# Gates of tokens 0 to 127 through a table in DRAM, written by accumulating scatter DMAs, in a kernel of two transformer blocks with PEER experts

## The chip, the cores and the metric

The kernel runs on one core of a Trainium2 chip. The time is the device time in microseconds (us), as a median of several runs; a profiled execution gives the trace. Engines are named as in the profile: PE (TensorE; PEld is its weight load), DVE (VectorE), ACT (ScalarE), POOL (GpSimd) and SP (SyncE, which here issues the loads of weights).

## The reference

256 tokens of width 1024 pass a first block (an attention and a gated linear recurrence, an FFN, a gate) and a second block: a mixer of two attentions, and then a PEER layer, which is the part that matters here.

```python
def peer_ffn(xn, w_peer_q, sub_keys, expert_u, expert_v):
    xt = xn.reshape(T, D)
    qh = (xt @ w_peer_q).reshape(T, PEER_HEADS, 2, PEER_HALF)      # 8 heads
    s = jnp.einsum('thpd,hpnd->thpn', qh, sub_keys)                # 128 keys a half
    sv, si = lax.top_k(s, PEER_TOPK)                               # 16
    cand = sv[:, :, 0, :, None] + sv[:, :, 1, None, :]
    cand_idx = si[:, :, 0, :, None] * PEER_NKEYS + si[:, :, 1, None, :]
    best, pick = lax.top_k(cand, PEER_TOPK)
    expert_idx = jnp.take_along_axis(cand_idx, pick, axis=-1)      # of 16384 experts
    gates = jax.nn.softmax(best, axis=-1)
    ...
    hval = jnp.einsum('cd,chkd->chk', xc, expert_u[ic])
    a = gc * jax.nn.gelu(hval, approximate=False)
    return jnp.einsum('chk,chkd->cd', a, expert_v[ic])
```

So each token has 8 x 16 = 128 pairs of an expert and a gate. Within a head a token's 16 experts differ; two heads may pick the same one, and their gates then add up.

## The kernel before

**Weights.** All weights come as units of 128 x 1024 float32 (0.5 MB), in one fixed order (plan, line 38). SP loads unit u into raw[u % 4] as soon as DVE is done with the unit four before it (weights, line 465). ACT rounds it to wh (high, line 1736), DVE makes the rest wl = raw - wh (low, line 655; the subtraction is line 665), and PE multiplies with both halves. ACT and DVE work some three units ahead of PE (LOOK = 3; in the expert_u phase DVE does low of two units ahead).

**The PEER layer, dense part.** Tokens 0 to 207 (TN = 208) are multiplied with all 16,384 experts: 128 blocks of expert_u, in the order ORDER, n = 0 to 127. The gelu of each product is multiplied by a gate that is zero where the token did not pick the expert, and the result goes through the 128 blocks of expert_v. The gates stand in one tile, gates[128, 128, 208]: the partition is the index j in a block, then comes the block i, then the token. The gelus of the first NP = 50 blocks are put in this tile while the gates don't exist yet (early, line 3121; gelu, line 2266).

**The gates.** DVE finds each token's picks beside the query weights and the first 50 blocks of expert_u: four sorts of the sub-keys for each half of the tokens (q = 0 and 1; line 1452), then for each q the pairs (pairs, ranks, at_rank: lines 1462 to 1518), which end in ij (i and j of each pick), and gain and gain_sum, which make the gates bst. ACT does the exp and copies keys for it at fixed blocks (at_keys, line 2299). Between them slot() (line 1442) does low of one weight unit. PE turns ij and bst over (line 3137), and from block 51 on a chunk of four tokens is built beside each block: DVE and ACT make one-hot tiles oj and oi (128 picks x 128, oi scaled by the gate), and PE multiplies them for each token, which gives all 16,384 gates of it in a bank (line 3155). DVE and ACT carry them from the bank into the tile gates, multiplied by the gelus that are there (lines 1636 and 2348). 208 tokens are NC = 52 chunks, at blocks 51 to 102. Blocks after 50 have their gelu multiplied by the part of the gates built so far (gated, line 1583; built, line 379).

**The few tokens.** Tokens 208 to 255 don't go through all experts. Their picks and gates are copied to DRAM and back (few_picks, pick), and POOL fetches rows of expert_u and expert_v with 2 x 48 indirect DMAs of 128 rows of 4 KB each (line 645). A row fetch j waits until fetch j - 3 was used, as there are three buffers. DVE uses them in slots (slot_taken, line 1596), a dot product or a multiply-add of 1024 elements. slots_taken (line 435) writes the places out:

```python
at = {GATED - 1 - 3 * k: SOON - 1 - k for k in range(SOON)}
for n in range(GATED, NE - 2, 2):
    at[n] = len(at)
```

That is slot 0 at block 57, then each third block to block 102, and each second from block 103; the rest in the expert_v phase. DVE works in the order in which these loops write it, so a slot whose row isn't there holds up all that stands behind it.

## Time and profile before

| | |
|---|---|
| median of 3 runs | 1323.21 us (1322.51 to 1324.47) |
| the profiled execution, its own time | 1321.23 us |
| its span in the trace | 1319.4 us |
| PE busy | 1298.7 us (98%) |
| DVE busy | 1069.2 us (81%) |
| ACT busy | 821.6 us (62%) |
| POOL busy | 226.9 us (17%), 151 instructions |
| DMA | 292.73 MB, mean 222 GB/s |

Times within the trace count from the start of its span. A matmul is pipelined, so the time of a stretch is read from the starts of the instructions in it and not from the sum of their durations. The span on POOL of a DMA that it issues is the time in which POOL builds it, not the transfer.

### The profile page before, as it was taken

Reading aid. Unit: us, or ns where it says so; the run is one execution under the profiler, and the core shown is the slowest. Engines: PE = TensorE matmul, PEld = TensorE weight load, DVE = VectorE, ACT = ScalarE, POOL = GpSimd, SP = SyncE. Lnnn points to the kernel's source line nnn. Section 1 sums busy time; section 2 is a strip of 40 time slices with the busy share of each in tenths; the row PEclk is TensorE's granted clock in tenths of the full one; section 3 lists DMA queues with packets and bytes.
Section 4 is the critical chain, followed back from the end, with each engine's and each line's share of the span. In section 5 each row is a group of like instructions: output and inputs, shape, how many; then the busy total and the mean of one; then the engine's idle time right before and its main releaser. Section 6 shows DMA issues by size and latency. Waiting matters only on the chain.

```text
span 1319.4 us, 21754 instructions
## 1 busy us (share of the span) xinstructions
PE 1298.7 (98%) x8061; PEld 1200.7 (91%) x8061; DVE 1069.2 (81%) x1974; ACT 821.6 (62%) x1601; POOL 226.9 (17%) x151
## 2 busy tenths in 40 slices
PE   8999999999999999999899999999999999999998
PEld 6998888888889888889899999999999999999995
DVE  6867776666677675778899889999999989988985
ACT  6886555555556555455466888888666555555553
POOL 3002030000000000000000021100334436545610
PEclk9999999999999999999899999999999999999999
DMA  6533365555535344654656655565788999999972
GB/s 228 182 120 136 113 223 192 186 187 189 183 136 176 128 144 166 232 190 155 183 202 220 208 211 208 200 210 200 271 304 325 366 344 361 369 364 342 349 281 91
DMA packets 82603, 292.73 MB, mean 222 GB/s; under 512 B 10217, under 2 KB 10873, under 8 KB 82242
## 3 DMA queue, kind: packets, MB, share of 16 engines
q1 hardware_dynamic: 68450, 240.70, 52.8%
q0 software_dynamic: 14048, 50.64, 10.4%
q8 instruction: 65, 1.06, 0.3%
q14 instruction: 40, 0.33, 0.1%
HBM read 288.95 MB, written 2.34 MB: 221 GB/s over the span
## 4 chain that ended last, share of the span: by engine, by line
PE 86%; DVE 7%; ACT 3%; DMA 3%; issue 2%; POOL 0%; SPq 0%; POOLq 0%; DVEq 0%; ACTq 0%
PE bank L2409 84%; DMA raw<-in_wts 3%; DVE wl L665 2%; PE bank L2507 1%; ACT wh L1748 1%; DVE rows L1604 1%; PE bank L2495 1%; DVE oi L1580 0%; DVE gates L1636 0%; DVE oj L1576 0%; DVE gates L1588 0%; ACT kdz L1754 0%; DVE St L855 0%; ACT oi L2329 0%; ACT oi L2333 0%
## 5 line engine op out<-in xcount | busy, mean ns | idle before, releaser
L2409 PE MATMUL bank<-hTb,wh 128*128 128x416 f32 (+3 forms) x2768 | 827.5, 363 | 3.4 <-DVE wl L665 3.2
L2409 PE MATMUL bank<-hTb,wl 128*128 128x208 f32 (+2 forms) x2584 | 652.7, 264 | 0.0
L665 DVE TENSOR_TENSOR wl<-raw,wh 128x1024 fp32r<-128x1024 f32 x429 | 523.9, 1228 | 133.8 <-ACT wh L1748 131.5
L1748 ACT ACTIVATE wh<-raw 128x1024 fp32r<-128x1024 f32 x429 | 449.8, 1057 | 205.5 <-PE bank L2409 118.3
L2409 PEld LDWEIGHTS bank<-hTb,wh 128*128 128x128 f32 (+1 forms) x2768 | 506.2, 189 | 26.0 <-issue 4.8
L2409 PEld LDWEIGHTS bank<-hTb,wl 128*128 128x128 f32 (+1 forms) x2584 | 492.7, 191 | 4.8
L2409 PE MATMUL bank<-wh,hTb 128*128 128x512 f32 (+2 forms) x552 | 175.0, 398 | 1.9 <-DVE hTb L699 1.9
L2409 PEld LDWEIGHTS bank<-wh,hTb 128*128 128x128 f32 (+1 forms) x552 | 102.2, 187 | 24.7 <-DVE wl L665 2.1
L645 POOL DMA_INDIRECT rows<-in_v_rows,pick x48 | 105.6, 2200 | 92.0 <-DVE acc L1615 76.8
L645 POOL DMA_INDIRECT rows<-in_u_rows,pick x48 | 74.3, 1548 | 229.5 <-DVE dots L1604 226.8
L2409 PE MATMUL bank<-wl,hTb 128*128 128x512 f32 (+2 forms) x276 | 100.3, 389 | 0.0
L563 POOL TENSOR_TENSOR st<-st,mhalf 128x1 f32<-128x1 f32 (+2 forms) x15 | 13.1, 877 | 501.5 <-DVE st L672 252.5
L1754 ACT ACTIVATE low_half<-bank 128x208 fp32r<-128x208 f32 x77 | 26.6, 345 | 62.5 <-PE bank L2409 62.1
L2409 PEld LDWEIGHTS bank<-wl,hTb 128*128 128x128 f32 (+1 forms) x276 | 51.6, 187 | 10.5
L1615 DVE SCALAR_TENSOR_TENSOR acc<-rows,factor,acc 128x1024 f32<-128x1024 f32 x46 | 58.9, 1280 | 0.0
L1604 DVE CUSTOM_DVE_ANT_0 rows<-rows,xr 128x1024 f32<-128x1024 f32 x48 | 58.6, 1222 | 0.0
L2409 PE MATMUL bank<-oi,oj 128*128 128x128 f32 x416 | 55.2, 276 | 0.0
L2409 PEld LDWEIGHTS bank<-oi,oj 128*128 128x128 f32 x416 | 52.5, 191 | 0.1
L2409 PE MATMUL bank<-wh,ab 128*128 128x512 f32 x168 | 48.5, 390 | 0.0
L1641 DVE TENSOR_TENSOR hTb<-gates,hTb 128x208 fp32r<-128x208 f32 x126 | 46.7, 371 | 0.0
L1754 ACT ACTIVATE hTb<-gates 128x208 fp32r<-128x208 f32 x126 | 45.5, 361 | 0.0
L2409 PEld LDWEIGHTS bank<-wh,ab 128*128 128x128 f32 x168 | 31.5, 188 | 5.9
(428 smaller groups left out, 1397.3 us busy)
## 6 DMA issues: line engine op xcount, KB each, us to landing
raw<-in_wts SPq DMA_DIRECT2D x441, 512.0 KB
x<-in_x SPq DMA_DIRECT2D x4, 256.0 KB, 4.8
sk<-in_sk SPq DMA_DIRECT2D x1, 1024.0 KB
spill<-x SPq DMA_DIRECT2D x1, 1024.0 KB
xr<-few_x SPq DMA_DIRECT2D x2, 512.0 KB
x<-spill SPq DMA_DIRECT2D x4, 256.0 KB
rows<-in_u_rows,pick POOLq DMA_INDIRECT x48
rows<-in_v_rows,pick POOLq DMA_INDIRECT x48
```

Source lines behind the costliest of these rows:

```text
L563: signal(e.tensor_tensor(o, ms, mhalf[:, 0:o.free_size()], ALU.pow), name)
L645: e.indirect_dma_start(out=rows[j % 3][:, :], out_offset=None, in_=I["u_rows"] if j < SLOTS else I["v_rows"], in_offset=bass.IndirectOffse ...
L665: e.tensor_tensor(b[:, :], raw[u % RAW][:, :], a[:, :].bitcast(F), ALU.subtract).then_inc(S("lo"), 1)
L1604: e.tensor_tensor_reduce(out=t[:, :], in0=t[:, :], in1=xr[:, g, :], scale=1.0, scalar=0.0, op0=ALU.mult, op1=ALU.add, accum_out=dots[:, k: ...
L1615: e.scalar_tensor_tensor(out=acc[:, g, :], in0=t[:, :], scalar=factor[:, k:k + 1], in1=acc[:, g, :], op0=ALU.mult, op1=ALU.add).then_inc(S ...
L1641: e.tensor_tensor(b, gates[:, ORDER[n], :], a.bitcast(F), ALU.subtract).then_inc(S("al"), 1)
L1748: e.activation(parts_of(u)[0][:, :], raw[u % RAW][:, :], ACT.Copy).then_inc(S("hi"), 1)
L1754: return e.activation(o, i, ACT.Copy)
L2409: return e.matmul(o, l, r, start=first, stop=last, skip_group_check=True)
L2495: p = e.transpose(B[turned_at(t, i)[0]][:, two(128, k)], src[:, q, 512 * j + 128 * k:512 * j + 128 * k + 128], ident[:, :])
L2507: p = e.transpose(b[:, two(128, k)], src(k), ident[:, :])
```

## The change

NS = 128: the gates of tokens 0 to 127 no longer come from one-hot products, so NC goes from 52 to 20 chunks (tokens 128 to 207), at blocks 49 to 68, and NP from 50 to 48.

- **The table.** gate_of in DRAM has 128 x 128 x 128 float32 (block, j, token), 8 MB. POOL zeroes it early, with 8 DMAs of 1 MB from the zeroed tile kTb.
- **The scatters.** After the pairs of the first 128 tokens, DVE (places) works out spots = (128 i + j) x 128 + token, as one column of 128 tokens for each of the 128 picks, and shares, the gates. POOL then issues 128 indirect DMAs, each of which adds one column of shares (128 numbers of 4 bytes) to the table at the column of spots. Before each head but the first it waits until all scatters so far have landed.
- **Order of DVE's work.** The last of the eight sorts (tops(7)), which is of the second half of the tokens, is moved behind the whole chain of the first half. gain, exp and gain_sum of the first half come with it; keys are copied at blocks 17, 18, 20, 22.
- **POOL's order.** few_picks is copied out at head 3 and the copies to pick are issued after its fourth scatter. 16 row fetches stand between the scatters, two after each eight, from the end of head 3 to the middle of head 7. The other row fetches follow after all scatters. The slots are now at blocks 60, 62, ... 118. The few tokens' x is copied by POOL (12 DMAs), not by SP.
- **Reading back.** SP loads the table in 16 parts of 8 blocks (0.5 MB, runs of 512 bytes), in its queue between the weight loads: before units 116 and 118 of expert_u, then before every fourth unit of expert_v from 0 to 52. The first waits for all 128 scatters. DVE multiplies each part into the gelus with one instruction (spread). high_of on ACT waits for the part it needs.
- **Blocks after 48.** gelu is split at token 128: only the 80 tokens above go through ga and gated. Some semaphores are merged (b_lo, b_hi, b_ps), and the first load of x counts on in_end.

```diff
-NP, NB = 50, 5
+NP, NB = 48, 5
-NC = TN // 4
+NS = 128
+NC = (TN - NS) // 4
+SPREAD = 8
+PICKED = 3
...
+        def loaded_at(m):
+            return NE - 12 + 2 * m if m < 2 else NE + 4 * (m - 2)
+        def spread_at(m):
+            return NE - 7 + 2 * m if m < 2 else NE + 4 * (m - 2)
...
-            at = {GATED - 1 - 3 * k: SOON - 1 - k for k in range(SOON)}
-            for n in range(GATED, NE - 2, 2):
-                at[n] = len(at)
+            at = {60 + 2 * k: k for k in range(30)}
...
+                    if u in at_load:
+                        gate_rows(at_load[u])
...
+            def gate_rows(m):
+                if m == 0:
+                    e.wait_ge(S("in_spread"), 16 * 128)
+                    e.wait_ge(S("G_ps"), NC)
+                if m >= 2:
+                    e.wait_ge(S("spread"), m - 1)
+                b = blocks_of(m)
+                e.dma_start(spread_in[m % 2][:, :, :], I["gate_of"].rearrange("(i j t) a -> i j (t a)", i=NE, j=128)[b]
+                            .rearrange("i j t -> j i t")).then_inc(S(f"in_gate{m % 2}"), 16)
...
+            empty = I["gate_of"].rearrange("(p a) b -> p (a b)", p=128)
+            for n in range(8):
+                copied(empty[:, two(2048, n)], kTb[:, :, :, :].rearrange("p a b c -> p (a b c)"))
...
+            fetched = 0
+            e.wait_ge(S("best"), 3)
+            for h in range(8):
+                if h == PICKED:
+                    e.wait_ge(S("best"), 8)
+                    copied(I["few_picks"], chosen[128 - FEW:128, :, :])
+                if h:
+                    e.wait_ge(S("in_spread"), 256 * h)
+                for k in range(16):
+                    if h == PICKED and k == 4:
+                        e.wait_ge(S("in_few"), 16 * 22)
+                        for g, t, a in ((0, slice(MORE, FEW), 4), (1, slice(0, MORE), 128 // MORE)):
+                            for i in range(2):
+                                copied(pick[:, i, slice(32 * g, 32 + MORE * g)],
+                                       I["few_picks"][t, i, :].rearrange("t (a k) -> a t k", a=a))
+                    p = 16 * h + k
+                    e.indirect_dma_start(
+                        out=I["gate_of"], out_offset=bass.IndirectOffsetOnAxis(ap=spots[:, p:p + 1], axis=0),
+                        in_=shares[:, p:p + 1], in_offset=None, compute_op=ALU.add).then_inc(S("in_spread"), 16)
+                    if h == PICKED and k == 12:
+                        e.wait_ge(S("in_few"), 16 * 26)
+                    if h >= PICKED and k in (7, 15) and h + k < 22:
+                        for _ in range(2):
+                            if (h, k) != (PICKED, 7):
+                                row(fetched)
+                                fetched += 1
+            for j in range(fetched, 2 * SLOTS):
+                row(j)
...
+            def spread(m):
+                b = blocks_of(m)
+                e.wait_ge(S("gelu"), SPREAD * m + SPREAD)
+                e.wait_ge(S(f"in_gate{m % 2}"), 16 * (m // 2 + 1))
+                e.tensor_tensor(gates[:, b, 0:NS], gates[:, b, 0:NS], spread_in[m % 2][:, :, :], ALU.mult).then_inc(S("spread"), 1)
...
             for q in range(2):
+                if q:
+                    tops(7)
                 pairs(q)
...
                 if q == 0:
                     at_rank(q, 1)
-            gain_sum(0)
+                    gain_sum(0)
+                    places()
             gain_sum(1)
```

## Rows read from the trace of the kernel before

**Rows 1.** The page, engines and the chain that ended last.

```profile
PE 1298.7 (98%) x8061; PEld 1200.7 (91%) x8061; DVE 1069.2 (81%) x1974; ACT 821.6 (62%) x1601; POOL 226.9 (17%) x151
...
PE 86%; DVE 7%; ACT 3%; DMA 3%; issue 2%; POOL 0%; SPq 0%; POOLq 0%; DVEq 0%; ACTq 0%
```

**Rows 2.** Stretches: length, busy us by engine, PE clock, DMA share, GB/s.

```profile
185.00:230.00 45.00, 45.00 (x240) 38.58 (x239) 31.66 (x44) 24.08 (x39) 4.39 (x6) 1.00 0.57 189
...
755.60:937.20 181.60, 180.37 (x1304) 178.50 (x1303) 173.55 (x371) 156.88 (x472) 23.82 (x22) 1.00 0.60 208
...
1000.00:1115.00 115.00, 115.00 (x769) 114.33 (x767) 101.87 (x146) 64.17 (x99) 52.89 (x27) 1.00 0.96 350
1115.00:1260.00 145.00, 145.00 (x969) 144.27 (x968) 131.44 (x159) 80.51 (x123) 79.83 (x37) 1.00 0.96 360
```

**Rows 3.** Instructions of PE in order of time, first and last chunk of 52.

```profile
752.38 0.26 PE L2409 MATMUL bank<-low_half,ones 128*128 128x208 f32 x1
...
758.15 1.07 PE L2409 MATMUL bank<-oi,oj 128*128 128x128 f32 x8
...
932.27 1.05 PE L2409 MATMUL bank<-oi,oj 128*128 128x128 f32 x8
```

**Rows 4.** The chain that ended last, 940 to 961.

```profile
940.65 9.93 PE bank L2409 x64
950.58 0.02 issue
950.60 9.93 PE bank L2409 x64
```

**Rows 5.** Instructions of DVE in order of time: start, us, what.

```profile
657.45 0.71 DVE L1422 MAX8 sv<-ss 128x8 f32<-128x128 f32 x3
...
665.52 0.34 DVE L1465 CAST sif<-si 128x256 f32<-128x256 uint32 x1
...
704.48 0.29 DVE L1513 TENSOR_TENSOR ij<-eq 128x128 f32<-128x128 bf16 x1
...
739.47 0.28 DVE L1529 TENSOR_REDUCE sm<-bst 128x8 f32<-128x128 f32 x1
...
748.17 0.29 DVE L1513 TENSOR_TENSOR ij<-eq 128x128 f32<-128x128 bf16 x1
...
939.28 1.23 DVE L665 TENSOR_TENSOR wl<-raw,wh 128x1024 fp32r<-128x1024 f32 x1
940.41 0.38 DVE L1588 TENSOR_TENSOR gates<-gates,ga 128x208 f32<-128x208 f32 x1
```

**Rows 6.** Instructions of POOL in order of time, with idle time before.

```profile
753.74 0.73 POOL L629 DMA_DIRECT2D pick<-few_picks  x1 [2.59 <-DMA few_picks<-chosen]
...
762.02 0.59 POOL L629 DMA_DIRECT2D pick<-few_picks  x1 [1.68 <-issue]
764.70 1.07 POOL L645 DMA_INDIRECT rows<-in_u_rows,pick  x1 [2.08 <-DMA pick<-few_picks]
766.07 0.98 POOL L645 DMA_INDIRECT rows<-in_u_rows,pick  x1 [0.30 <-issue]
767.36 1.34 POOL L645 DMA_INDIRECT rows<-in_u_rows,pick  x1 [0.30 <-issue]
...
794.13 0.93 POOL L645 DMA_INDIRECT rows<-in_u_rows,pick  x1 [7.74 <-DVE dots L1604]
...
939.36 1.96 POOL L645 DMA_INDIRECT rows<-in_u_rows,pick  x1 [2.40 <-DVE dots L1604]
```

**Rows 7.** DMA issues of POOL: KB each, median us to landing.

```profile
few_picks<-chosen POOLq DMA_DIRECT2D x1, 48.0 KB, 2.8
...
pick<-few_picks POOLq DMA_DIRECT2D x2, 8.0 KB, 2.2
```

**Rows 8.** GB/s in 40 slices of the stretch 764 to 800.

```profile
GB/s 32 278 273 177 378 300 209 241 391 396 405 314 146 300 255 0 187 378 18 0 177 387 18 0 0 223 414 419 401 291 0 132 391 73 5 118 350 373 323 55
```

**Rows 9.** Line 1604: ns min/median/max, first and last start.

```profile
L1604 DVE CUSTOM_DVE_ANT_0 rows<-rows,xr x48: 1217/1220/1236, 782.9 to 1077.0; 128x1024 f32<-128x1024 f32 x48
```

**Rows 10.** Groups of POOL, 1000 to 1260: busy us, mean ns, idle before.

```profile
L645 POOL DMA_INDIRECT rows<-in_v_rows,pick x47 | 103.4, 2199 | 91.4 <-DVE acc L1615 76.1 <-DVE dots L1604 7.6 <-DVE acc L1612 6.7
```

More of the change, by code:

```diff
@@ L423, in x_part @@
         def x_part(q, n):
-            return ("x00", "later", "peer", "out")[2 * q + n]
+            return ("end", "later", "peer", "out")[2 * q + n]
         def used_by(j):
@@ L1451, in vector, with tops @@
             both(ahead[0] - 5)
-            for i in range(8):
+            def tops(i):
                 q = i % 2
@@ L1460, in vector @@
                         slot()
+            for i in range(7):
+                tops(i)
             def pairs(q):
```

158 lines of the change are left out of this document (88 added, 70 removed).

## The prediction

> **What bounds the kernel now.** I read the page first, then the chain of waits, then the stretches by stage, then the instructions in order of time on POOL and DVE. The page says that PE is busy for 98% of the span and is 86% of the chain that ended last [rows 1]: an edit gains only where it takes PE time away, and loses wherever it makes PE wait. So I ask of each stretch how much PE works, and who is close behind it [rows 2]. In the stretch of the one-hot products (755.6 to 937.2) DVE has 173.55 us of work in 181.6 and PE 180.37: both are full. In the blocks after it (940.65 on) the chain is PE alone. In the expert_v phase (1000 to 1260) PE never stops, DVE is busy for 233.3 us of 260, and the DMA engines show a share of 0.96. POOL, by contrast, only fetches rows, with long idle times between: this is where the change puts 128 new instructions.
>
> **What is removed.** The products of the first chunk are issued at 758.15 and those of the 52nd at 932.27 [rows 3]: 174.12 / 51 = 3.414 us for a block of expert_u with a chunk. In the chain, four blocks without one (64 matmuls) take 9.93 us, and the next four begin 9.95 after the first [rows 4]: 2.486 us a block. 32 chunks go: 32 x (3.414 - 2.486) = **-29.7 us**. This takes in the one-hots on DVE and ACT and the copies out of PSUM, since it compares whole blocks; the DVE and ACT waits in the chain of that stretch are part of the 3.414. NP = 48 instead of 50 only moves the start: two blocks without a chunk come after it instead of before it. The transposes wait for "best" 6, and DVE is done with the indices at 748.2 + 0.3 [rows 5], about when PE gets there (its last matmul ahead of them is at 752.38 [rows 3], less two blocks of 2.5: 747.4): 1 us, in the term "else" below.
>
> **What is added on POOL.** 128 scatters, of 128 single numbers each, one after the other. The trace has no accumulating scatter. The nearest rows are the gathers of line 645, which also take 128 indices from SBUF. The first three wait for nothing between them: 1.07, 0.98 and 1.34 us with 0.30 between, 1.43 us from one to the next [rows 6]. Alone, one takes 0.93 to 0.94; 1.96 where DVE has just begun a subtraction with two inputs in SBUF: DVE's runs from 939.28 and the next begins 1.13 later, POOL's starts at 939.36 and ends 0.9 after that [rows 5, 6]. Bounds for one scatter T, its gap included: below, 0.59 + 0.30 = 0.89 (the shortest direct DMA; it reads no index), with 0.94 + 0.30 = 1.24 the floor if it is built like a gather; above, 2.20 + 0.30 = 2.50 (the mean gather in the expert_v phase [rows 10]). I take 1.43: unblocked gathers beside DVE work like that of 700 to 930.
>
> The Trainium skill, page "SBUF — State Buffer", section "Who interferes with whom", says that a DVE instruction with two inputs in SBUF contends with a GpSimd instruction that reads SBUF. The 0.93 against 1.96 agrees; by the bare floor T would be 1.24 and by its rule taken for every scatter 2.26.
>
> POOL's timetable:
> - Start. The chain of the first 128 tokens on DVE ends at 704.8; tops(7), from 657.5 to 665.5, moves behind it, so 696.7 [rows 5]; gain, gain_sum and places are some nine short instructions like that of 739.47 (0.28), +2.3: **699**.
> - Heads 0 to 2: 48 x 1.43 = 68.6, and two waits for a landing. The nearest landing in DRAM from POOL is few_picks, 2.8 us [rows 7]: 5.6. At **773.2** "best" 8 (750) is long there.
> - Head 3: landing 2.8, few_picks 0.5 + 0.3, 16 scatters 22.9, the four copies to pick as before 8.9 (753.74 to 762.61, idle times with them [rows 6]), two row fetches 2.9: **811.6**.
> - Then seven times 8 scatters and 2 row fetches, 14.3 each, and four landings of 2.8: 111.3, **922.9**. The last of the 16 rows lands some 2.5 later, between the 2.2 and 2.8 of rows 7: **925.4**.
>
> Who waits for that: DVE takes slot k at block 60 + 2k, so slot 15 at block 90, and DVE works in program order; behind it stand the low halves that PE needs two blocks later. Due time: slot 0 of before stands at block 57 (chunk 6, products at 758.15 + 6 x 3.414 = 778.6) and is taken at 782.9 [rows 9], 4.3 behind. After the change chunk 0 stands two blocks earlier (753.1), chunk 19 at 818.0, block 90 at 818.0 + 22 x 2.486 = 872.7, its slot at **877.0**. POOL is late by 925.4 - 877.0 = **48.3 us**, and all of it becomes a wait of DVE and then of PE. It builds up from slot 0 on (block 60, due 795.0, its row not before 812). The loads of the table stand in SP's queue before unit 116 and wait for all scatters (922.9 + 11.4 + 2.8 = 937); unit 116 would be loaded about 923 + 48, so this wait is covered, but if the slots did not stall it would be the next to bind, past about 925. SP's weight loads are queued behind it. The 16 row fetches of POOL lie in the sum; the rest come as before.
>
> **What is added in the expert_v phase.** 14 of 16 table loads of 0.52 MB, by the 46th block of it, say 115 us: 7.3 MB, 64 GB/s on top of 350 [rows 2]. Single slices of 0.9 us reach 414 to 419 GB/s [rows 8], so it may just fit: cost 0 at best, (350 + 64) / 360 x 115 - 115 = 17 at worst (with the 360 GB/s of rows 2 as the ceiling). The runs are 512 bytes where others are 4 KB; no row prices that. DVE gets 14 multiplications of 1,024 elements, 1.23 each like that of 939.28: 17 us, beside 115 - 101.9 = 13 idle in that stretch; part shows. I take **+5**. The two in the expert_u phase stand beside shorter gate multiplications (80 columns, not 208).
>
> **Else.** Zeroing: 8 MB from 185 us on, beside the weights; the share of the DMA engines is 0.57 there at 189 GB/s [rows 2], so 8.4 MB find room in some 50 us: 0 at best, 5 if the weights come late behind a burst. xr comes by 12 small copies of POOL from 623 on, idle till 699: nothing. With the start: **+1**.
>
> **Sum**, against the profiled execution's 1321.2: -29.7 + 48.3 + 5 + 1 = +24.6, so 1345.8; the median stands 2.0 above that execution: **1348 us**. In the way to slot 15 stand 48 + 16 + 2 + 70 = 136 instructions at T. So 0.18 us less (T = 1.25) brings the sum to zero; 0.1 us is worth 13.6.
>
> **Rivals.**
> 1. POOL keeps pace: a scatter moves 4 bytes, and may be cheaper than a gather. Place: slot 15. At T = 1.20 the lateness is 17 and the sum -7 (1316); at 1.08 and below it is gone and -29.7 + 5 + 1 = -24 remain (1299); with nothing lost in the expert_v phase 1294. It decides from T = 1.25 down. For it: 0.59 for direct DMAs. Against: no indexed DMA in the rows is under 0.93, and the gap of 0.30 stands even where nothing is waited for.
> 2. The scatter is dearer: it must read the old number too, or DVE blocks each. At T = 2.26, lateness 48.3 + 136 x 0.83 = 161, about 1461; at 1.80, about 1398. For it: the gather of 1.96 and the mean of 2.20 in the expert_v phase. The Trainium skill, page "DMA: Bandwidth & Descriptors", section "Anatomy of one DMA — SWDGE (gpsimd) path", gives a DMA of this path about 2.0 us of fixed time, mostly completion. If that were paid each time and not once a head, T = 2.0 and the time about 1425; the 1.43 of the first three gathers speaks against that, since they overlap.
> 3. The floor exactly, T from 1.21 to 1.31: 1318 to 1332, gain and stall cancel.
> 4. POOL keeps pace, but the table loads are bound by the DMA engines: -29.7 + 17 + 1, 1311.
>
> **Chances.** Forecast (T 1.32 to 1.80: 1333 to 1398) 0.38; dearer 0.17; floor 0.10 (0.02 faster, 0.04 same, 0.04 slower); rivals 1 and 4 together 0.35. Faster by over 0.2% (about what a measurement tells from no change) 0.37, same 0.04, slower 0.59. Range 1296 to 1405: it leaves out nearly all of the dear case and the lowest end. The likeliest case alone: 1333 to 1398.
>
> **What would show it.** Right: POOL solid from 699 to about 935 with instructions of 0.94 to 1.34; DVE idle before the dot products of line 1604 for rows from block 60 on, about 48 us in sum; PE idle behind low halves in the same place; blocks of 2.49 us from block 69 if the wait is taken off; some more waiting for weights from 970 to 1110. Wrong: a T far from 1.43; a start of the scatters later than 700; landings well over 2.8 at the head waits; DMA waits of PE in the expert_v phase of over 10 us.

## The result, and the profile after

| | |
|---|---|
| the changed kernel | 1535.72 us, median of 4 runs (1533.75 to 1538.96) |
| the kernel before, same chip | 1323.84 us, median of 4 runs (1322.51 to 1325.89) |
| ratio | 1.1598, 95% interval 1.158 to 1.1616: slower by 16% |
| predicted | 1348 us, 1296 to 1405 |

It is slower, and the waits are those of the prediction (DVE for rows, PE for DVE), but the time is 188 us longer than forecast, far outside the range.

The page of the changed kernel, engines and the chain that ended last, which answers [rows 1]:

```profile
PE 1294.5 (84%) x7784; PEld 1187.4 (77%) x7784; DVE 1041.8 (68%) x1886; ACT 786.4 (51%) x1490; POOL 451.4 (29%) x300
...
PE 54%; POOL 15%; issue 12%; DMA 8%; DVE 7%; ACT 3%; SPq 0%; POOLq 0%; ACTq 0%; DVEq 0%
```

PE's busy time is that of before to 4 us, in a span that is 218 us longer. It is not the same work: 277 matmuls are gone, and the rest took longer, as the clock below shows. Its share of the chain fell from 86% to 54%. What came in is POOL with 15% and "issue" with 12%: time in which POOL waits for nothing that the profile shows.

Stretches of the changed kernel, with the columns of [rows 2]:

```profile
185.00:230.00 45.00, 41.71 (x217) 34.70 (x216) 27.27 (x38) 21.67 (x35) 9.73 (x15) 1.00 0.91 350
755.60:937.20 181.60, 64.37 (x445) 63.67 (x445) 56.05 (x125) 56.39 (x183) 108.30 (x70) 0.67 0.33 65
830.00:1100.00 270.00, 99.86 (x551) 96.96 (x552) 78.95 (x151) 57.57 (x153) 165.75 (x107) 0.65 0.41 92
```

In the stretch where PE was busy for 180.37 us before [rows 2], it is now busy for 64.37. From 830 to 1100 it works 99.86 us of 270, and the granted clock is 0.65 in the mean, between its two levels of 1.2 and 2.4 GHz, where it was 1.00 with PE always busy. All engines are idle most of the time but POOL, and POOL has 166 us of 270.

The waits of the changed kernel: who waited for whom, us in total, times, longest:

```profile
PE bank L2500 <- DVE wl L728: 224.0, 16, 104.7
PEld bank L2500 <- ACT gates L2369: 223.3, 13, 104.9
DVE rows L1689 <- DMA rows<-in_u_rows,pick: 216.6, 9, 104.8
```

The third row is the cause of the first two: DVE stands at a dot product for 216.6 us, in nine waits, for rows that POOL has not asked for. These are three of the nine, on DVE in order of time:

```profile
900.15 1.22 DVE L1689 CUSTOM_DVE_ANT_0 rows<-rows,xr 128x1024 f32<-128x1024 f32 x1 [104.85 <-DMA rows<-in_u_rows,pick]
928.10 1.22 DVE L1689 CUSTOM_DVE_ANT_0 rows<-rows,xr 128x1024 f32<-128x1024 f32 x1 [12.57 <-DMA rows<-in_u_rows,pick]
...
1113.94 1.22 DVE L1689 CUSTOM_DVE_ANT_0 rows<-rows,xr 128x1024 f32<-128x1024 f32 x1 [14.54 <-DMA rows<-in_u_rows,pick]
```

Slot 0 comes 104.85 us late, and then every second slot some 14 more, since POOL sends two rows after each eight scatters.

And this is why. POOL in order of time, the first scatters (DVE and PE busy), some of the third head (both stopped), and the rows:

```profile
699.90 1.72 POOL L699 DMA_INDIRECT gate_of<-shares,spots  x1 [67.19 <-DVE spots L1611]
701.92 2.09 POOL L699 DMA_INDIRECT gate_of<-shares,spots  x1 [0.30 <-issue]
704.31 1.84 POOL L699 DMA_INDIRECT gate_of<-shares,spots  x1 [0.31 <-issue]
709.87 1.75 POOL L699 DMA_INDIRECT gate_of<-shares,spots  x1 [3.71 <-issue]
...
829.31 1.55 POOL L699 DMA_INDIRECT gate_of<-shares,spots  x1 [1.82 <-issue]
831.16 1.54 POOL L699 DMA_INDIRECT gate_of<-shares,spots  x1 [0.30 <-issue]
833.01 1.54 POOL L699 DMA_INDIRECT gate_of<-shares,spots  x1 [0.30 <-issue]
836.50 1.56 POOL L699 DMA_INDIRECT gate_of<-shares,spots  x1 [1.95 <-issue]
...
847.23 1.55 POOL L699 DMA_INDIRECT gate_of<-shares,spots  x1 [0.30 <-issue]
...
896.08 1.02 POOL L679 DMA_INDIRECT rows<-in_u_rows,pick  x1 [0.30 <-issue]
...
1083.09 1.00 POOL L679 DMA_INDIRECT rows<-in_u_rows,pick  x1 [0.30 <-issue]
```

Two things stand in these rows. A scatter takes 1.53 us at the least, where a gather took 0.93 to 1.34 [rows 6]. And after three scatters with 0.30 between them comes a pause that has no releaser, 1.7 us at the least and up to 5.5.

The pauses go by count. In heads 0 to 2 they stand before scatters 4, 7, 10 and so on to 46, every third, and there is a second series before 8, 15, 22, 29, 36 and 43, every seventh. A wait for all landings doesn't start the count again. POOL makes such a wait before the 33rd scatter, and the pause before the 34th comes all the same:

```profile
810.10 1.55 POOL L699 DMA_INDIRECT gate_of<-shares,spots  x1 [1.67 <-DMA gate_of<-shares,spots]
813.58 1.54 POOL L699 DMA_INDIRECT gate_of<-shares,spots  x1 [1.93 <-issue]
```

So a pause does not mean that three scatters are on their way at that moment. The group as the page has it:

```profile
L699 POOL DMA_INDIRECT gate_of<-shares,spots x128 | 221.2, 1728 | 226.2 <-issue 152.5
```

The mean is 1.73 us, and of the 226.2 idle 67.2 lie before the first. So a scatter took 1.728 + (226.2 - 67.2) / 128 = **2.97 us**, where the prediction had 1.43.

### The profile page after: what moved, and what is told of

Same layout as the page of the kernel before. It is cut to its first block, busy times and chain, and to the rows that moved or that the text cites. A ratio compares the mean times of both kernels' runs of the same rounds, so it can differ in the third digit from the quotient of the medians.

```text
span 1537.2 us, 21199 instructions
## 1 busy us (share of the span) xinstructions
PE 1294.5 (84%) x7784; PEld 1187.4 (77%) x7784; DVE 1041.8 (68%) x1886; ACT 786.4 (51%) x1490; POOL 451.4 (29%) x300
## 4 chain that ended last, share of the span: by engine, by line
PE 54%; POOL 15%; issue 12%; DMA 8%; DVE 7%; ACT 3%; SPq 0%; POOLq 0%; ACTq 0%; DVEq 0%
PE bank L2500 52%; POOL gate_of L699 14%; DMA raw<-in_wts 6%; DVE wl L728 4%; ACT wh L1838 1%; PE bank L2598 1%; POOL rows L679 1%; DVE rows L1689 1%; DMA rows<-in_v_rows,pick 1%; DMA gate_of<-shares,spots 1%; PE bank L2586 1%; DVE acc L1700 0%; DVE hTb L1727 0%; DMA rows<-in_u_rows,pick 0%; DMA x<-in_x 0%
## 5 line engine op out<-in xcount | busy, mean ns | idle before, releaser
L2500 PE MATMUL bank<-hTb,wh 128*128 128x416 f32 (+3 forms) x2768 | 843.6, 369 | 226.8 <-DVE wl L728 221.0
L2500 PEld LDWEIGHTS bank<-hTb,wh 128*128 128x128 f32 (+1 forms) x2768 | 514.8, 192 | 257.1 <-ACT gates L2369 223.3
L2500 PE MATMUL bank<-hTb,wl 128*128 128x208 f32 (+2 forms) x2584 | 661.1, 267 | 0.0
L2500 PEld LDWEIGHTS bank<-hTb,wl 128*128 128x128 f32 (+1 forms) x2584 | 503.3, 195 | 4.9
L699 POOL DMA_INDIRECT gate_of<-shares,spots x128 | 221.2, 1728 | 226.2 <-issue 152.5
L1689 DVE CUSTOM_DVE_ANT_0 rows<-rows,xr 128x1024 f32<-128x1024 f32 x48 | 58.6, 1220 | 216.6 <-DMA rows<-in_u_rows,pick 216.6
L2366 ACT ACTIVATE ga<-us 128x80 f32<-128x80 f32 (+5 forms) x69 | 17.5, 254 | 190.2 <-DVE us L1680 190.2
L679 POOL DMA_INDIRECT rows<-in_u_rows,pick x48 | 69.6, 1449 | 117.4 <-DVE dots L1689 111.5
L1844 ACT ACTIVATE us<-bank 128x208 f32<-128x208 f32 x69 | 23.6, 342 | 89.2 <-PE bank L2500 81.7
L1680 DVE TENSOR_TENSOR us<-bank,us 128x208 f32<-128x208 f32 x69 | 25.6, 371 | 33.9 <-ACT us L1844 33.1
```

The source lines that it names most:

```text
L679: e.indirect_dma_start(out=rows[j % 3][:, :], out_offset=None, in_=I["u_rows"] if j < SLOTS else I["v_rows"], in_offset=bass.IndirectOffse ...
L699: e.indirect_dma_start(out=I["gate_of"], out_offset=bass.IndirectOffsetOnAxis(ap=spots[:, p:p + 1], axis=0), in_=shares[:, p:p + 1], in_of ...
L1680: e.tensor_tensor(u, B[2 + n % 4][:, 0:TN], u, ALU.add).then_inc(S("u_sum"), 1)
L1689: e.tensor_tensor_reduce(out=t[:, :], in0=t[:, :], in1=xr[:, g, :], scale=1.0, scalar=0.0, op0=ALU.mult, op1=ALU.add, accum_out=dots[:, k: ...
L1844: return e.activation(o, i, ACT.Copy)
L2366: e.activation(ga[n % 4][:, 0:c], b[:, NS:NS + c], ACT.Gelu)
```

## The experiments

The time of the kernel before is given as it was measured beside each group of runs: 1325.99 us (no_scatter, no_scatter_no_loads, plain_scatter), 1324.8 (ring_3072, ring_3072_plain, xr_only, no_zeroing), 1325.8 (half_indices, half_heads, tokens_64), 1325.96 (the last two). Where one run is named there is no interval; executions of the kernel before spread from 1321.59 to 1333.07 in one such group, so a difference of a few us from a single run says little.

**No scatters.** Is everything but POOL's lateness as predicted?

```diff
-                    e.wait_ge(S("in_spread"), 16 * 128)
...
-                if h:
-                    e.wait_ge(S("in_spread"), 256 * h)
...
-                    e.indirect_dma_start(
-                        out=I["gate_of"], out_offset=bass.IndirectOffsetOnAxis(ap=spots[:, p:p + 1], axis=0),
-                        in_=shares[:, p:p + 1], in_offset=None, compute_op=ALU.add).then_inc(S("in_spread"), 16)
```

> Leaves out the 128 scatters and the waits for them, so the table holds zeros and the gates of tokens 0 to 127 are zero; all else, with the 16 loads of the table, stays. If the whole loss is POOL's lateness at the row fetches, what is left is the sum of the other terms, -29.7 + 5 + 1 = -24: 1300 us (0.982 of before), and 1294 to 1312 by the bounds. If the table loads or the moved sorts cost more than I counted, it comes out above 1312.

Measured 1306.3 us (1303.29 to 1309.21), ratio 0.9868 [0.984, 0.9896], 19.7 less than before. So the scatters and what waits for them cost 1535.7 - 1306.3 = 229 us. Its engines, from its page, for a comparison below:

```profile
PE 1273.5 (98%) x7784; PEld 1166.7 (90%) x7784; DVE 1041.2 (80%) x1886; ACT 786.4 (60%) x1490; POOL 237.4 (18%) x172
```

**No table loads either** (14 of 16 parts aren't loaded; two are, and are used for all):

```diff
                 if m >= 2:
-                    e.wait_ge(S("spread"), m - 1)
+                    return
...
-                e.wait_ge(S(f"in_gate{m % 2}"), 16 * (m // 2 + 1))
+                e.wait_ge(S(f"in_gate{m % 2}"), 16)
```

> Leaves out the scatters and 14 of the 16 table loads; DVE still multiplies 16 times, always with the first two parts (zeros). Against the run without scatters alone this prices the loads in the expert_v phase: 0 to 17 us by my bounds, 5 taken, so about 1295. A rival: the 512-byte runs are dear, and the difference is over 20 us.

Measured 1301.66 us (1299.53 to 1303.34), ratio 0.9822 [0.9795, 0.985]. The 14 loads cost 1306.3 - 1301.66 = 4.6 us, and the multiplications beside them stay in both. In the traces the expert_v phase, from the first ab<-gates to the first fold, takes 961.3 to 1267.9 = 306.6 us with them and 967.6 to 1267.4 = 299.8 without, a difference of 6.8. The two profiled executions as a whole differ by 0.55 only (1303.29 and 1302.74), since the blocks between the last chunk and that phase took 6.2 us more in the one without loads, where the two programs are alike. So the price of the loads is some 5 to 7 us and not known better. The kernel before also takes 299.8 us for that phase (985.9 to 1285.7), so the multiplications cost nothing that shows.

**Plain scatters**, which write and don't add (where two heads of a token picked the same expert, one gate is lost):

```diff
-                        in_=shares[:, p:p + 1], in_offset=None, compute_op=ALU.add).then_inc(S("in_spread"), 16)
+                        in_=shares[:, p:p + 1], in_offset=None).then_inc(S("in_spread"), 16)
```

> The scatters overwrite and don't accumulate: an expert that two heads picked keeps only the last gate. 128 instructions with the same indices and waits. Theory A, that the accumulation itself is dear because the old number has to be read as well: POOL's 1.54 us falls to about 0.94, the gaps after every third scatter go or come seldomer, T falls from 3.1 in the first heads to 1.3 or 1.4, and the time to about 1340. Rival B, that any indexed write of 4 bytes costs this: 1.54 and the gaps stay and the time stays near 1535.

Measured 1396.69 us (one run). Tile gate_of (ns min/median/max, first and last start), and POOL in order of time:

```profile
L699 POOL DMA_INDIRECT gate_of<-shares,spots x128: 953/997/3437, 699.6 to 968.2; - x128
```

```profile
699.59 1.08 POOL L699 DMA_INDIRECT gate_of<-shares,spots  x1 [67.18 <-DVE spots L1611]
...
709.78 0.96 POOL L699 DMA_INDIRECT gate_of<-shares,spots  x1 [0.30 <-issue]
714.15 1.51 POOL L699 DMA_INDIRECT gate_of<-shares,spots  x1 [3.42 <-issue]
```

Without the addition the scatter is the gather's price, 0.96, and the pause comes after the **seventh** (709.78), not after the third; the next ones come before scatters 15, 22, 29, 36 and 43, which is the second series of the change. Adding costs POOL 0.58 us an instruction at the least (0.52 in the mean, 1.211 against 1.728), and something that takes seven plain scatters takes only three adding ones.

```profile
L699 POOL DMA_INDIRECT gate_of<-shares,spots x128 | 155.0, 1211 | 151.3 <-issue 77.8
```

Theory A was right in kind, but its 1340 was 57 us too low: a plain scatter takes 1.211 + (151.3 - 67.2) / 128 = 1.87 us with its pauses, and not 1.3 or 1.4.

**A larger ring.** POOL's DMAs are described in a space of 1024 bytes a partition, set by one number of the program. It was made three times as large; ra and rc, two small tiles of an early stage, lie on the memory of a larger one to make room. With 4096 bytes, which was meant first, the tiles did not fit in SBUF, so there is no time for it.

```diff
-            ra = M("ra", [128, 2, 4, 32])
-            rc = M("rc", [128, 2, 4, 32])
+        HOST = M.p
+            ra = sb("ra", [128, 2, 4, 32], F, HOST)
+            rc = sb("rc", [128, 2, 4, 32], F, HOST + 1024)
...
-    nc = bacc.Bacc("TRN2", target_bir_lowering=False, num_devices=1, dynamic_dma_scratch_size=1024)
+    nc = bacc.Bacc("TRN2", target_bir_lowering=False, num_devices=1, dynamic_dma_scratch_size=3072)
```

> The changed kernel with 3072 bytes of descriptor space a partition for POOL's DMAs instead of 1024 (two small tiles of the FFN share other memory to make room; nothing else differs). Theory ring: the pauses after every third scatter are waits for room in the ring of descriptors, which holds three accumulating scatters at 1024 bytes, so it holds some 11 here. The pauses inside a head go away but for those after the eleventh; one scatter costs 1.84 to 2.0 us, heads 0 to 2 take about 48 x 2.0 + 3 x 3 = 105 instead of 147 us, the rows come about 100 us earlier, and the time is 1400 to 1450. Rival rate: the pauses show what the DMA engines need for one accumulating scatter of 128 numbers, 2.4 us, whatever the room; then the pauses only move behind the eleventh scatter or into the landing at each head, heads 0 to 2 take 130 to 147 us, and the time stays over 1490. Rival neither: the pauses are of POOL itself, nothing changes, 1536.

Measured 1444.95 us (1444.2 to 1446.87), ratio 1.0908 [1.0874, 1.0943]: 91 us less than the change from this number alone. POOL in order of time; the last row is the twelfth scatter:

```profile
700.73 1.71 POOL L700 DMA_INDIRECT gate_of<-shares,spots  x1 [67.21 <-DVE spots L1612]
...
724.47 1.81 POOL L700 DMA_INDIRECT gate_of<-shares,spots  x1 [0.30 <-issue]
730.62 1.54 POOL L700 DMA_INDIRECT gate_of<-shares,spots  x1 [4.34 <-issue]
```

Eleven in a row, then the pause, and again before scatters 23, 34 and 45, every eleventh; the second series stands before 22 and 43. Three in 1024 bytes and eleven in 3072: if a pause comes when the next scatter doesn't fit, one adding scatter of 128 numbers takes over 3072 / 12 = 256 and at most 3072 / 11 = 279 bytes (an estimate from these counts); a plain one, seven in 1024, between 128 and 146. What the profile calls "issue" here goes with the room. Since the counts run on through the waits for all landings, the room seems to be given back once for each time round the ring, and not as each scatter lands. That is read from the places of the pauses in heads 0 to 2 and wasn't tried by itself; from scatter 65 on, with row fetches between, this run has no pause at all, and why is open.

Heads 0 to 2 took 119 us and not the 105 expected, 2.5 a scatter, with six pauses left. The rival rate had put the time over 1490. It has this against it too: if the DMA engines needed 2.4 us for each scatter and POOL sent ten in 20 us, some would still be waiting at the head, but the waits for landing there are 3.02, 2.87 and 1.12 us, no longer than the 3.54, 1.67 and 1.28 of the change.

The Trainium skill, page "Collectives: The Full Stack", section "The bandwidth ceiling: the fold count and why AG ≠ RS ≠ AR", says of a transfer that adds that it needs two descriptors on the reading side for each piece, since it reads two sources, where a copy needs one. The counts here, three against seven, agree. The page "DMA: Bandwidth & Descriptors", section "SWDGE vs HWDGE vs iDMA", places the rings that GpSimd writes in SBUF; that SBUF had to be found for a larger one agrees.

**Both together.**

> As ring_3072, and the scatters write instead of adding (where two heads of a token picked the same expert, one gate is lost). Theory ring: all 16 scatters of a head follow each other with 0.30 between, 1.27 us each where DVE and PE are quiet and up to 1.7 where they are busy; against plain_scatter's 1397 it gains another 15 to 40 us: 1355 to 1380. Rival rate: no gain over plain_scatter, 1397.

Measured 1369.52 us (one run), within the range of the theory; 27 less than plain_scatter. In heads 0 to 2 the only pauses are those before scatters 22 and 43.

**Half the numbers in each scatter** (the gates of tokens 64 to 127 are left out of the table):

```diff
-                        out=I["gate_of"], out_offset=bass.IndirectOffsetOnAxis(ap=spots[:, p:p + 1], axis=0),
-                        in_=shares[:, p:p + 1], in_offset=None, compute_op=ALU.add).then_inc(S("in_spread"), 16)
+                        out=I["gate_of"], out_offset=bass.IndirectOffsetOnAxis(ap=spots[0:64, p:p + 1], axis=0),
+                        in_=shares[0:64, p:p + 1], in_offset=None, compute_op=ALU.add).then_inc(S("in_spread"), 16)
```

> The changed kernel with 128 accumulating scatters of 64 numbers each, not 128 (the gates of tokens 64 to 127 are left out of the table). Theory: POOL writes descriptors at a rate, so span and room go with their number; by plain_scatter (0.96 us, seven in flight) against the change (1.54, three in flight), half the numbers of an adding scatter are as many descriptors as a plain one of 128: 0.96 us, a pause after every seventh, and the time of plain_scatter, 1380 to 1410. Rival fixed: adding itself costs 0.6 us on POOL and 8 places, whatever the count; then 1.3 to 1.5 us, a pause after three to five, 1450 to 1520.

Measured 1456.56 us (one run): the time is the rival's. POOL in order of time, scatters seven and eight:

```profile
711.54 2.07 POOL L699 DMA_INDIRECT gate_of<-shares,spots  x1 [0.30 <-issue]
717.31 2.37 POOL L699 DMA_INDIRECT gate_of<-shares,spots  x1 [3.70 <-issue]
```

```profile
L699 POOL DMA_INDIRECT gate_of<-shares,spots x128: 1389/1414/4140, 699.2 to 1025.6; - x128
```

Here the theory was half wrong. The room does go with the count: seven go out before a pause, as with the plain ones of 128. The time on POOL hardly does: 1.39 us at the least against 1.53, so the 0.58 for adding is not paid by the number. A scatter of half the size saves room and little time.

**The scatters of heads 0 to 3 alone** (heads 4 to 7 are left out of the table):

```diff
-                    e.wait_ge(S("in_spread"), 16 * 128)
+                    e.wait_ge(S("in_spread"), 16 * 64)
...
-                if h:
+                if 0 < h < 5:
                     e.wait_ge(S("in_spread"), 256 * h)
...
+                    if h < 4:
                         e.indirect_dma_start(
```

> The changed kernel with the scatters of heads 0 to 3 alone (64 of them; the gates of heads 4 to 7 are left out of the table). Theory: DVE waits for slot 0's row as long as in the change, 105 us, since the first three heads are as before, and then never again: no_scatter's 1306 plus 105, 1411, with one long wait of DVE in place of nine. Rival: the stall comes from the load of the table at unit 116 or from DMA load and not from the rows; then the time stays over 1450 or falls by less than 100.

Measured 1413.96 us (one run), 3 from the theory. Its waits:

```profile
DVE rows L1690 <- DMA rows<-in_u_rows,pick: 106.9, 1, 106.9
```

One wait in place of nine. 1306.3 + 106.9 = 1413.2, so a late row costs its lateness once. (no_scatter's own executions spread from 1303.29 to 1309.21, so the agreement to 1 us is in part luck.)

The runs with scatters side by side. "Over" is what remains of the profiled execution's span after no_scatter's 1301.6 and DVE's wait; the last column is how much longer PE is busy than in no_scatter, with the same 7784 matmuls (1273.5 us there, 1294.5 in the change):

| | time | DVE waits for rows | over | PE busy longer by |
|---|---|---|---|---|
| the change | 1535.7 | 216.6, 9 times | 19.0 | 21.0 |
| half_indices | 1456.6 | 131.6, 9 times | 21.6 | 21.9 |
| ring_3072 | 1445.0 | 122.7, 9 times | 18.6 | 19.4 |
| half_heads | 1414.0 | 106.9, once | 3.7 | 3.0 |
| plain_scatter | 1396.7 | 79.3, 9 times | 14.1 | 16.9 |
| ring_3072_plain | 1369.5 | 50.3, 7 times | 15.9 | 14.7 |

The wait explains each span to 22 us, and to 4 where it is a single wait. What is over goes with the last column, to 3 us in each of the six: after each wait the same matmuls run at a lower clock (0.65 in the mean from 830 to 1100 of the change), and nine short waits cost more of that than one long one. No run held the clock up, so this is a match of six pairs of numbers and not a trial.

**The few tokens' x alone.** The kernel before, with x by POOL's 12 small copies instead of two broadcast loads in SP's queue, one part of the change that was priced at nothing:

```diff
-            fetch(xr[:, 0, :], bc(I["few_x"][MORE:FEW, :], 0, 4), "peer")
-            fetch(xr[:, 1, :], bc(I["few_x"][0:MORE, :], 0, 128 // MORE), "peer")
...
+            for g, t in ((0, slice(MORE, FEW)), (1, slice(0, MORE))):
+                m = t.stop - t.start
+                for a in range(128 // m):
+                    copied(xr[two(m, a), g, :], I["few_x"][t, :])
```

> The kernel before with one thing of the change: the few tokens' x comes by 12 small copies of POOL, not by two broadcast loads in SP's queue. Theory: the two loads held up the weights behind them near 640, PE ran 16 us of 20 there at a clock of 0.83; without them 3 to 6 us are regained, 1320 to 1323 where the kernel before takes 1326. Rival: the DMA engines were late for another reason in that stretch, and nothing changes.

Measured 1318.04 us (1315.72 to 1320.05, 8 runs), ratio 0.9943 [0.9921, 0.9965]: 6.8 us less than before, a little more than the theory's 3 to 6. The stretch 640 to 660, of the kernel before and then of this one:

```profile
640.00:660.00 20.00, 16.03 (x91) 15.62 (x92) 16.86 (x71) 10.81 (x22) 0.00 (x0) 0.83 0.53 185
```

```profile
640.00:660.00 20.00, 20.00 (x137) 19.89 (x136) 20.00 (x85) 12.19 (x24) 0.00 (x0) 1.00 0.64 210
```

Three more rows of the kernel before, which the prediction did not read: a piece of the chain that ended last, ACT's wait for it, and a stretch of 3 us in it.

```profile
627.41 14.62 DMA raw<-in_wts
```

```profile
ACT wh L1748 <- DMA raw<-in_wts: 6.8, 1, 6.8
```

```profile
632.00:635.00 3.00, 3.00 (x23) 2.98 (x22) 3.00 (x14) 1.65 (x4) 0.00 (x0) 1.00 1.03 176
```

The first load of weights behind the two broadcasts was issued as soon as its buffer was free and took 14.62 us to land, and ACT stood for 6.8 of them. The DMA engines were full in that time and moved 176 GB/s, where they move 360 at a share of 0.96 in the expert_v phase [rows 2]. So it is the broadcasts themselves that were slow. The run changes their shape and their queue at once; which of the two helps was not taken apart.

**No zeroing**, in the kernel without scatters and loads (its two parts come from the weights):

```diff
-            for n in range(8):
-                copied(empty[:, two(2048, n)], kTb[:, :, :, :].rearrange("p a b c -> p (a b c)"))
...
```

> As no_scatter_no_loads, and the table isn't zeroed either (the two parts that are still loaded come from the weights, with 4 KB runs). Theory: the eight DMAs of 1 MB hold up the weights at 186 to 215 and cost 6 us, so 1296 against no_scatter_no_loads' 1302. Rival: they only take slack that PE loses anyway, no more than 1 us.

Measured 1295.49 us (1293.12 to 1298.1), ratio 0.9778 [0.9752, 0.9803]: 6.2 us less than no_scatter_no_loads, or 5.0 if each is taken against the kernel before beside it, and that is what the zeroing costs. The stretch 185 to 230 here (the change has 41.71 us of PE in it, above), and the matmuls of the chunks, with their first and last start:

```profile
185.00:230.00 45.00, 45.00 (x237) 38.26 (x236) 30.95 (x45) 24.76 (x40) 5.22 (x7) 1.00 0.61 193
```

```profile
L2490 PE MATMUL bank<-oi,oj x160: 272/275/289, 749.7 to 814.3; 128*128 128x128 f32 x160
```

The first chunk comes at 749.7 and not at 753.8 as in no_scatter_no_loads, 4.1 us earlier.

And this is how the change issues the eight DMAs:

```profile
186.10 3.99 POOL L603 DMA_DIRECT2D gate_of<-kTb  x7 [0.32 <-POOL kTb L582]
214.67 0.54 POOL L603 DMA_DIRECT2D gate_of<-kTb  x1 [24.58 <-issue]
```

Seven go out in 4 us and the eighth after a pause of 24.58 us without a releaser; in ring_3072 all eight go out between 185.50 and 190.03. So the room for seven plain DMAs of POOL shows here too.

**A version meant to win.** Only tokens 0 to 63 go through the table, and their 64 x 128 gates are packed two picks to a column, so that 64 scatters of 128 numbers do it, eight a head, in a ring of 2560 bytes.

```diff
-NS = 128
-SPREAD = 8
+NS = 64
+SPREAD = 16
...
+            for v in (spots, shares):
+                w = v[:, :].rearrange("p (h k) -> p h k", h=8)
+                copied(w[64:128, :, 0:8], w[0:64, :, 8:16])
...
-                for k in range(16):
+                for k in range(8):
...
-            at = {60 + 2 * k: k for k in range(30)}
+            at = {63 + 3 * k: k for k in range(8)}
+            at.update({86 + 2 * k: 8 + k for k in range(20)})
```

> A version meant to win: only tokens 0 to 63 go through the table, 36 chunks by one-hots. The upper eight picks of each head are moved to partitions 64 to 127 by two small copies, so that 64 adding scatters of 128 numbers do it, eight a head; the ring has 2560 bytes, room for nine. The table is 4 MB, loaded in 8 parts of 16 blocks. Slots 0 to 7 at every third block from 63, the next 20 at every second from 86. Theory: 16 chunks go, 16 x 0.928 = -14.9; x by POOL's copies -6.8 (xr_only); zeroing half of 6, +3; half the loads, +2.3: 1324.8 - 16.4 = 1308, if POOL keeps up: 699 + 4 + 64 x 2.3 + landings 20 + rows 25 = 895, slot 8 not due before 878 and its row sent at 851. Rival late: POOL is some 10 us late at slots 0 to 2 already (due at 801, rows sent at 790 if a scatter costs 2.2, at 800 if 2.6), and 5 to 10 us come back: 1313 to 1320. Rival DVE: blocks from 85 on take 2.77 and not 2.49 us with a slot in every second, as in no_scatter_no_loads: +12, 1320.

Measured 1322.77 us (1320.59 to 1327.86, 12 runs), ratio 0.9988 [0.9973, 1.0003]: no gain. But POOL kept up:

```profile
L705 POOL DMA_INDIRECT gate_of<-shares,spots x64: 1538/1726/3767, 700.9 to 873.3; - x64
```

172.4 us for 64 scatters, the copies and the first nine rows, and DVE doesn't wait for a row once. The gain went in three places, read against xr_only: the first chunk's products start at 751.2 and not at 752.2 less two blocks of 2.5, so it is 4 us late; the 43 blocks after the last chunk (870.5 to 974.7) take 104.2 us where xr_only's 25 take 53.5 (926.8 to 980.3), so the 18 more cost 2.82 each and not 2.49, 6 us; and from there to the first fold it takes 310.1 us where xr_only takes 300.4, 10 us. Of the first 4 us the zeroing has some 1.5: no_zeroing, which zeroes nothing, starts its first chunk at 749.7. In the kernels with a table PE also waits 1.5 us for ACT (tile gates) near 700, and in before and xr_only it doesn't. The third place and then the first are taken on by the next runs.

**Long runs in the table.** The table by j, block, token instead of block, j, token (places works out the spots to match): a part is read in runs of 4096 bytes a partition, not 256.

```diff
-    I["gate_of"].rearrange("(i j t) a -> i j (t a)", i=NE, j=128)[b].rearrange("i j t -> j i t")
+    I["gate_of"].rearrange("(j i t) a -> j i (t a)", i=NE, j=128)[:, b]
```

> tokens_64 with the table laid out by j first, then block, then token, so that a part of 16 blocks is read in runs of 4096 bytes a partition and not 256. Theory: in tokens_64 the expert_v phase, from the first ab<-gates (974.7) to the first fold (1284.8), took 310 us where xr_only took 300.4; the short runs of the table loads are the cause of at least half of that, so 4 to 6 us less: 1317 to 1319. Rival: the bytes and the eight multiplications cost it, not the length of the runs; then no more than 1 us, 1322.

Measured 1319.05 us (1314.34 to 1320.66), ratio 0.9945 [0.9926, 0.9963]: 3.7 less, a little under the theory and over the rival. In the traces the expert_v phase takes 307.7 us (975.1 to 1282.8) and not 310.1, 2.4 less; it is still 7.3 over xr_only's 300.4, and what makes up that rest is open. The stretch 1000 to 1115, short runs and then long ones:

```profile
1000.00:1115.00 115.00, 109.22 (x708) 105.40 (x707) 97.38 (x138) 56.94 (x88) 50.09 (x25) 1.00 0.98 347
```

```profile
1000.00:1115.00 115.00, 111.50 (x729) 108.31 (x728) 100.36 (x141) 58.67 (x90) 51.67 (x26) 1.00 0.96 358
```

More is moved in less of the DMA engines' time: 347 GB/s at a share of 0.98 became 358 at 0.96, and PE gets 2.3 us more to do.

**Zeros one after the other**, with the long runs; the loop stands a few instructions later than the burst did:

```diff
-            for n in range(8):
-                copied(empty[:, two(2048, n)], kTb[:, :, :, :].rearrange("p a b c -> p (a b c)"))
...
+            for n in range(16):
+                if n:
+                    e.wait_ge(S("in_few"), 16 * n)
+                copied(empty[:, two(512, n)], kTb[:, :, :, :].rearrange("p a b c -> p (a b c)")[:, 0:512])
```

> tokens_64_long_runs, and the table is zeroed by 16 DMAs of 0.25 MB, each issued when the one before has landed, from 193 us on while POOL is idle until 357. Theory: in tokens_64 the burst of 4 MB at 186 made the weights late, and the first chunk came 4 us later than it would have; with one piece in flight the weights keep their pace: 3 to 4 us less than tokens_64_long_runs, 1314 to 1316, which would beat xr_only (1318). Rival: the bytes take their share of the DMA engines wherever they lie, or the delay is not of the zeroing; no gain.

Measured **1313.56 us** (1310.82 to 1317.68, 6 runs), ratio 0.9911 [0.9891, 0.9932]: 5.5 less than with the burst, faster than both kernels, by 12.4 us or 0.9% against before. Of the 12.4 some 6.8 are those of x (xr_only); against xr_only's ratio of 0.9943 [0.9921, 0.9965] the table itself gains some 4 us, and as the two intervals overlap that is not sure. The stretch 185 to 230 of tokens_64_long_runs, and of this one:

```profile
185.00:230.00 45.00, 44.44 (x232) 37.56 (x231) 30.05 (x45) 24.16 (x40) 7.19 (x11) 1.00 0.80 287
```

```profile
185.00:230.00 45.00, 45.00 (x237) 38.28 (x236) 31.42 (x44) 24.31 (x39) 9.75 (x15) 1.00 0.72 241
```

The same bytes are spread over a longer time (from 190.1 to beyond 256.8, and seven of the sixteen pieces are issued behind this stretch), and PE is never out of work. The first chunk comes 1.9 us earlier (749.4 for 751.3), the first ab<-gates 3.0 (972.1 for 975.1) and the first fold 3.8 (1279.0 for 1282.8). The two profiled executions differ by these 3.8; the 5.5 are of the medians.

## Why the prediction was wrong, point by point

**The step that failed is T, the price of a scatter: "I take 1.43".** It measured 2.97 over all (above), and both its bounds, 0.89 and 2.50, lay below. By the prediction's own timetable the rows of slots 14 and 15 are sent by 922.9; they were sent by 1084.40 + 0.97 = 1085.4. 120 scatters stand before them, so each took 162.5 / 120 = 1.35 us more than 1.43, and a little more still, since the landings took less than forecast. The rest of the sum holds: 1306.3 and the measured wait of 216.6 make 1522.9, within 13 of the time.

Two things make up the 1.54 between 2.97 and 1.43. The three gathers that gave the 1.43 had a mean of 1.13 and a gap of 0.30 [rows 6]; the scatters have a mean of 1.73, so 0.60 is POOL's own work, nearly all of it the addition (0.52 in the mean against plain_scatter). And in the place of the gap of 0.30 stand (226.2 - 67.2) / 128 = 1.24, so 0.94 is pauses (0.05 of it the waits for landings at the heads). The first is what rival 2 named ("it must read the old number too"). The second is in no rival.

The three gathers could not show it, and the prediction read them as if they could. They "wait for nothing between them", and that is so; but a burst of three is as long as the ring allows with adding scatters, and never long enough with plain ones. Pauses of this kind did stand in the trace of before, between the four small copies to pick, the second of them in [rows 6]. The copies as they are there, and then in ring_3072:

```profile
759.06 1.29 POOL L629 DMA_DIRECT2D pick<-few_picks  x2 [4.59 <-issue]
762.02 0.59 POOL L629 DMA_DIRECT2D pick<-few_picks  x1 [1.68 <-issue]
```

```profile
830.63 1.90 POOL L604 DMA_DIRECT2D pick<-few_picks  x3 [0.87 <-issue]
```

The prediction took the 8.9 us of the four as a fixed block, "idle times with them", and did not ask what the idle times were. Nor were the 1024 bytes of ring in the kernel's last lines weighed, which the change leaves as they are. The rule of the Trainium skill on the shared port (page "SBUF — State Buffer", section "Who interferes with whom"), which the prediction weighed, was the smaller matter: with DVE stopped the scatter still takes 1.54. Rival 2 gave 1461 for T = 2.26; by its own slope, 136 us for each us of T, 2.97 gives 1348 + 136 x 1.54 = 1557, 22 over what came.

**The start**, 699: 699.90. Right.

**The waits at the heads**, 2.8 each: in all 6.5 us in three waits (3.54, 1.67 and 1.28); from head 4 on two row fetches stand before the wait, and the last scatters land beside them. Small.

**Who waits for whom**: right. DVE at the slots, PE behind DVE's low halves for 224 us, from slot 0 on. The load of the table was not the next to bind: it starts at 1164.3, 55 us after the last scatter.

**The removal**, -29.7: it came to about -22. no_zeroing, which has neither scatters nor loads nor zeroing, is 29.3 below before, and 6.8 of that is x. In its trace the 59 blocks after the last chunk take 145.4 us (814.3 to 959.7), xr_only's 25 take 53.5, so the 34 more take 2.70 each (2.63 and 2.81 by the traces of no_scatter and no_scatter_no_loads, whose program is the same there). 34 x 0.21 = 7.3 us are lost. The 2.486 of [rows 4] is true of the four blocks in which it was measured. The stretch 940 to 960 of before and of xr_only, and 900 to 920 of no_scatter, all after the last chunk:

```profile
940.00:960.00 20.00, 19.96 (x131) 19.18 (x130) 18.67 (x33) 12.47 (x24) 7.64 (x5) 1.00 0.87 322
```

```profile
940.00:960.00 20.00, 18.54 (x122) 17.83 (x121) 17.86 (x31) 12.13 (x23) 6.35 (x5) 1.00 0.85 291
```

```profile
900.00:920.00 20.00, 18.57 (x123) 18.00 (x122) 16.62 (x30) 12.31 (x32) 6.53 (x4) 1.00 0.89 298
```

All three have a slot in every second block there, so the slots alone don't make the difference, and xr_only, with the blocks of before, is short of work as well. In no_scatter ACT waits 13.5 us for weights from 825 to 960, at a DMA share near 0.90. That rows and weights together are too much for the DMA engines over a long stretch is argued from this, and wasn't tried. A price read from four blocks was the best case of it.

**The expert_v phase**, +5: 4.6 by the medians of no_scatter and no_scatter_no_loads, 6.8 by that phase in their traces. Right as far as it can be told, though all of it is the loads and none of it the multiplications. The 512 byte runs, which "no row prices", are in it; with 256 byte runs in tokens_64 the length cost 3.7.

**Else**, +1, "0 at best, 5 if the weights come late": the zeroing took 5 to 6.2. That 8.4 MB find room in 50 us was true of the mean share and not of the moment: seven DMAs of 1 MB issued within 4 us take their share at once, and the weights issued after them come late (the DMA share is 0.91 from 185 to 230, PE has 41.71 us of work in 45). The 1 us for the start of the chunks was about right: the transposes wait 0.2 us for ij, and PE loses 1.5 us near 700, where it waits for ACT. And x "nothing": 6.8 us gained. The row was there to be read, 14.62 us of the chain at 627.41.

So the sum without lateness, -23.7, met a measured -19.7, but only as 6.8 that was missed on the one side stood against 7.3 and 5.2 (6.2 less the 1) on the other. That it came out near is luck.

## What to carry to other kernels

Before a price per instruction is multiplied by 128, ask whether the trace shows a burst as long as the new one, and what finite thing it would fill: here the ring of POOL's descriptors, one number in the program and 91 us. An adding indirect DMA of 128 numbers takes POOL 1.53 us at the least and about twice the room of a plain one, so use few, fill all 128 partitions, and put nothing that another engine waits for behind them in a timetable without slack. A large transfer that is wanted much later should be cut in pieces, one in flight at a time, and not be issued as a burst beside a stream of weights; and a load that broadcasts few rows over 128 partitions is best kept away from the critical loads. A price per block is better read from the longest stretch there is than from four blocks.

## What the runs showed of the hardware that was not expected

- An adding scatter of 128 numbers of 4 bytes takes POOL 1.53 us at the least and a plain one 0.95; of 64 numbers, adding, 1.39. The time is mostly fixed.
- In 1024 bytes of descriptor space three adding scatters of 128 go out before a pause, seven plain ones, seven adding ones of 64, and seven direct DMAs of 1 MB; in 3072 bytes eleven adding ones of 128. The pauses have no releaser in the trace and are called issue. They come by count, every third or eleventh, and go on so after a wait for all landings; adding scatters pause in a second series as well, every seventh, where the plain ones pause. With 2560 bytes and eight a head, 36 scatters followed each other from 783.88 on with only row fetches between and no pause, which the count doesn't explain.
- After two broadcast loads of 0.5 MB the next load of weights took 14.62 us to land, with the DMA engines full at 176 GB/s; the same bytes by 12 small copies of another queue held up nothing.
- Zeroing 4 MB by four DMAs at once cost 5.5 us more than by 16 one after the other (3.8 in the profiled executions).
- In six runs with the same 7784 matmuls PE was busy for 3.0 to 21.9 us longer than without the waits, about what the time was over the sum of waits.
